# RWKV's inverse updates summed in PSUM and copied by ScalarE, its preparation off GpSimd, and its steps earlier in the layer's script

## What is computed

```
h = rms_norm(x, norm_g[i]); z = h @ w_in[i]
y_a = rwkv7_branch(z_a, ...)      # 6 heads of 64
y_b = dsa_branch(z_b, ...)        # 4 heads, keys chosen by top-k of an index score
y_c = dilated_branch(z_c, ...)    # 6 heads, three masks, one joint softmax
x = x + concatenate([y_a, y_b, y_c]) @ w_out[i]
...
# rwkv7: state step per token
sa = einsum('bhvk,bhk->bhv', state, -kk_t)
state = state * w_t + sa[..., None] * (kk_t * a_t) + v_t[..., None] * k_t
y_t = einsum('bhvk,bhk->bhv', state, r_t)
```

## Time and profile before

| what | value |
|---|---|
| median of 3 runs | 1381.98 us (1381.41 to 1382.36) |
| the profiled execution's own time | 1390.62 us |
| its span | 1388.8 us |
| PE, DVE, ACT, POOL busy | 85%, 69%, 49%, 10% of the span |
| mean granted clock of PE | 0.896 |
| layer 0 of the first block | from the start to about 241 us |
| layer 1 of the first block | about 308 to 529 us |

### The profile page before, as it was taken

How to read it: one execution, slowest core, us unless ns; L and a number is a source line. 1 busy time by engine, 2 the same in 40 slices (tenths; PEclk the granted TensorE clock), 3 DMA queues, 4 the chain that set the end, 5 groups by cost and what they waited for, 6 DMA issues and landing times.

```text
span 1388.8 us, 24893 instructions
## 1 busy us (share of the span) xinstructions
PE 1174.7 (85%) x10397; PEld 1089.9 (78%) x10397; DVE 957.5 (69%) x1729; ACT 675.3 (49%) x1224; POOL 139.9 (10%) x140
## 2 busy tenths in 40 slices
PE   7879876979799759859967799997979869999796
PEld 6868665978688648758955599996978849999696
DVE  5677865666877856676768667887547476788752
ACT  5543233456442234555437656655444364565541
POOL 2011000110110001151000011111011001011100
PEclk9889966989899878979968999998989869999898
DMA  8333200344242004315430054554534303455450
GB/s 331 120 102 107 93 2 1 130 144 152 89 149 92 2 1 167 127 71 208 141 114 1 17 193 156 183 171 170 177 123 175 125 1 122 152 183 169 154 179 31
DMA packets 24448, 167.55 MB, mean 121 GB/s; under 512 B 2704, under 2 KB 2832, under 8 KB 8336
## 3 DMA queue, kind: packets, MB, share of 16 engines
q1 hardware_dynamic: 24336, 165.96, 34.1%
HBM read 164.90 MB, written 1.05 MB: 119 GB/s over the span
## 4 chain that ended last, share of the span: by engine, by line
PE 46%; DVE 33%; ACT 14%; issue 5%; DMA 1%; POOL 1%; POOLq 0%; DVEq 0%; SPq 0%; ACTq 0%
DVE WL L381 8%; PE ps L427 8%; PE ps L424 7%; PE ps L422 7%; DVE ARENA L2031 5%; DVE FR L381 4%; ACT WH L368 3%; PE ps L445 3%; PE ps L453 3%; PE ps L447 3%; ACT ARENA L745 2%; PE ps L643 2%; ACT FR L368 2%; DVE ARENA L2023 2%; DMA raw<-wst_in 1%
## 5 line engine op out<-in xcount | busy, mean ns | idle before, releaser
L381 DVE TENSOR_TENSOR WL<-raw,WH 128x1024 fp32r<-128x1024 f32 (+4 forms) x225 | 269.5, 1219 | 145.5 <-ACT WH L368 144.9
L422 PE MATMUL ps<-FR,WH 128*128 128x256 f32 x1248 | 313.7, 290 | 29.1 <-ACT WH L368 15.3
L424 PE MATMUL ps<-FR,WH 128*128 128x256 f32 x1248 | 310.6, 288 | 2.6 <-POOL FR L501 0.9
L368 ACT ACTIVATE WH<-raw 128x1024 fp32r<-128x1024 f32 (+4 forms) x225 | 217.5, 989 | 122.0 <-PE ps L427 65.1
L422 PEld LDWEIGHTS ps<-FR,WH 128*128 128x128 f32 x1248 | 246.9, 198 | 35.0 <-ACT WH L368 11.3
L424 PEld LDWEIGHTS ps<-FR,WH 128*128 128x128 f32 x1248 | 246.4, 197 | 6.2 <-POOL FR L501 2.1
L427 PE MATMUL ps<-FR,WL 128*128 128x256 f32 x1248 | 175.1, 284 | 10.5 <-DVE WL L381 10.5
L422 PE MATMUL ps<-FR,FR 128*128 128x256 f32 x680 | 170.4, 287 | 8.9 <-ACT FR L497 7.4
L424 PE MATMUL ps<-FR,FR 128*128 128x256 f32 x680 | 169.6, 286 | 0.9 <-DVE FR L501 0.7
L427 PEld LDWEIGHTS ps<-FR,WL 128*128 128x128 f32 x1248 | 160.9, 195 | 11.2 <-DVE WL L381 11.2
L381 DVE TENSOR_TENSOR FR<-raw,FR 128x1024 fp32r<-128x1024 f32 (+2 forms) x100 | 117.4, 1193 | 75.6 <-ACT FR L368 75.5
(11 more groups left out here) (308 smaller groups left out, 1820.2 us busy)
## 6 DMA issues: line engine op xcount, KB each, us to landing
raw<-wst_in SPq DMA_DIRECT2D x123, 1024.0 KB, 5.0
raw<-wst_in SPq DMA_DIRECT2D x17, 896.0 KB, 4.6
raw<-wst_in SPq DMA_DIRECT2D x11, 768.0 KB, 4.3
raw<-wst_in SPq DMA_DIRECT2D x4, 912.0 KB, 4.6
cst<-cst_in SPq DMA_DIRECT2D x1, 1681.0 KB, 15.0
X<-xT_in SPq DMA_DIRECT2D x2, 512.0 KB, 6.2
ARENA<-memT_in SPq DMA_DIRECT2D x1, 1024.0 KB, 5.5
out_dram<-X SPq DMA_DIRECT2D x2, 512.0 KB, 2.6
```

Of the source, the lines that this page charges most:

```text
L368: a.activation(hi[:, 0:cols], src, ACT.Copy).then_inc(*put("split_hi", ("hi", i)))
L381: v.tensor_tensor(lo[:, 0:cols], src, hi[:, 0:cols].bitcast(F32), SUB).then_inc(*put("split_lo", ("lo", i)))
L422: pe.matmul(out, hv[:, k, :], src.hi[:, c, :], start=k0 == 0 and k == ks[0], stop=False)
L424: pe.matmul(out, hv[:, k, :], src.lo[:, c, :], start=False, stop=False)
```

## The change

1. Updates: for each T and U update PE first adds minus the identity times the old T (or U) into the same place of PSUM, then the product. ACT copies the sum out with scale -1. DVE's subtractions go. A constant `minus i64` of 64 columns is added, and the arena is 64 columns smaller.
2. POOL's three products of the preparation and its start of U (as two instructions per half, the first a product with -1 and the mask) go to DVE.
3. For jobs 0 to 7 of both layers ACT multiplies P by 1/l (an activation with that scale); the reciprocal stays on DVE.
4. RWKV has two more steps (one before the transposes for PE and ACT; on DVE the Newton steps, the products behind them, and the last products are steps of their own), and the script places them otherwise: 34 of the 43 stand in the written part, 9 between the attention jobs.

```diff
-                   rows 2 0, gact 1, R, rows 2 1, gact 2, R, rows 2 2, R, rows 2 3, R, rows 3 0, rout 2, R, rows 3 1, ropei, R, rows 3 2, R,
...
+                   rows 2 0, gact 1, R, R, rows 2 1, gact 2, R, rows 2 2, R, R, rows 2 3, R, rows 3 0, rout 2, R, rows 3 1, ropei, R, R,
...
 # attn_v
-            if j.turn == "A":
+            if j.turn == "A" and "times" not in j.more:
                 for p, l in j.scales():
                     v.tensor_scalar(p, p, l, None, MUL).then_inc(*put("attn_v", ("P", j.id)))
 # attn_a
-        if s == 2 and j.turn == "V":
+        if s == 2 and (j.turn == "V" or "times" in j.more):
 # rwkv_pe
+                for x in ("T", "U") if lv < 5 else ("U",):
+                    ps, old = begin_bank(x, l, lv, b), m.Tm if x == "T" else m.Um
                     for i in range(6):
+                        u = 6 * b + i
                         for h in HALVES:
+                            pe.matmul(ps[h, 64 * i:64 * i + 64], MINUS[h, :], old[h, u, :], start=True, stop=False)
+                        for h in HALVES:
+                            w, r0 = (m.Um, m.Wm) if x == "T" else (m.Wm, m.Um)
+                            ins = pe.matmul(ps[h, 64 * i:64 * i + 64], w[h, u, :], r0[h, u, :], start=False, stop=True)
 # rwkv_a
+                for x, to in (("T", m.Tm), ("U", m.Um)) if lv < 5 else (("U", m.Um),):
...
+                    a.activation(to[:, us, :], six(ps), ACT.Copy, scale=-1.0).then_inc(*put("rwkv_a", (x, l, lv, b), free))
 # rwkv_v
+        v.tensor_tensor(g_, g_, m.tmp, MUL).then_inc(*put("rwkv_v", ("g", l)))
         newton(v, q, "rwkv_v", m.tmp, m.tmp, 0.0, m.kq)
+        yield
+        v.tensor_tensor(m.bq, m.bq, m.E2, MUL).then_inc(*put("rwkv_v", ("bq", l)))
+        v.tensor_tensor(m.kr[:, :, 1, :], r_, m.cs, MUL).then_inc(*put("rwkv_v", ("rq", l)))
+            v.scalar_tensor_tensor(m.Um[:, us, :], m.Mb[:, us, 0:64], -1.0, bc(C("level0t"), 1, 6), MUL, MUL).then_inc(*put("rwkv_v"))
+            v.tensor_tensor(m.Um[:, us, :], m.Um[:, us, :], bc(I64, 1, 6), ADD).then_inc(*put("rwkv_v", ("U", l, 0, b)))
-                    v.tensor_tensor(m.Tm[:, us, :], m.Tm[:, us, :], six(ps), SUB).then_inc(*put("rwkv_v", ("T", l, lv, b), free))
-                v.tensor_tensor(m.Um[:, us, :], m.Um[:, us, :], six(ps), SUB).then_inc(*put("rwkv_v", ("U", l, lv, b), free))
```

More of the change, by code:

```diff
@@ L50, in const_table @@
     parts["i64"] = k == n64
+    parts["minus i64"] = -1.0 * (k == n64)
     def rows(m):
@@ L1149, in rwkv_a @@
         yield
-        for _ in range(10):
+        for lv in range(1, 6):
+            yield
+            for b in range(2):
+                us = slice(6 * b, 6 * b + 6)
+                for x, to in (("T", m.Tm), ("U", m.Um)) if lv < 5 else (("U", m.Um),):
+                    ps, free = psum(x, l, lv, b)
+                    q.wait_ge(*got(x + " pe", l, lv, b))
+                    if x == "U":
+                        q.wait_ge(*got("U", l, lv - 1, b))
+                    a.activation(to[:, us, :], six(ps), ACT.Copy, scale=-1.0).then_inc(*put("rwkv_a", (x, l, lv, b), free))
             yield
@@ L1268, in rwkv_v @@
         yield
+        for b in range(2):
+            us = slice(6 * b, 6 * b + 6)
+            q.wait_ge(*got("M", l, "b", b, 1))
+            q.wait_ge(*got("prep pe", l))
+            v.scalar_tensor_tensor(m.Um[:, us, :], m.Mb[:, us, 0:64], -1.0, bc(C("level0t"), 1, 6), MUL, MUL).then_inc(*put("rwkv_v"))
+            q.wait_ge(*own("rwkv_v"))
+            v.tensor_tensor(m.Um[:, us, :], m.Um[:, us, :], bc(I64, 1, 6), ADD).then_inc(*put("rwkv_v", ("U", l, 0, b)))
         yield
@@ L1359, in rwkv_g @@
         m = lm[l]
-        r_, gate = m.zm[:, 0:3, :], m.zm[:, 9:12, :]
-        yield
-        q.wait_ge(*got("sg g", l))
-        g_.tensor_tensor(gate, gate, m.tmp, MUL).then_inc(*put("rwkv_g", ("g", l)))
-        yield
-        for _ in range(4):
-            yield
-        q.wait_ge(*got("b", l))
-        q.wait_ge(*got("e2", l))
-        g_.tensor_tensor(m.bq, m.bq, m.E2, MUL).then_inc(*put("rwkv_g", ("bq", l)))
-        yield
-        q.wait_ge(*got("e1", l))
-        q.wait_ge(*got("z", l, 2))
-        g_.tensor_tensor(m.kr[:, :, 1, :], r_, m.cs, MUL).then_inc(*put("rwkv_g", ("rq", l)))
-        yield
-        for _ in range(7):
-            yield
-        for b in range(2):
-            us = slice(6 * b, 6 * b + 6)
-            q.wait_ge(*got("M", l, "b", b, 1))
-            q.wait_ge(*got("prep pe", l))
-            g_.tensor_tensor(m.Um[:, us, :], m.Mb[:, us, 0:64], bc(C("level0t"), 1, 6), MUL).then_inc(*put("rwkv_g"))
-            q.wait_ge(*own("rwkv_g"))
-            g_.tensor_tensor(m.Um[:, us, :], bc(I64, 1, 6), m.Um[:, us, :], SUB).then_inc(*put("rwkv_g", ("U", l, 0, b)))
-        yield
-        for _ in range(12):
+        gate = m.zm[:, 9:12, :]
+        for _ in range(30):
             yield
```

39 lines of the change are left out of this document (17 added, 22 removed).

## The result

| | before | changed |
|---|---|---|
| median of 7 runs each | 1382.36 us | 1391.57 us |
| the profiled execution's own time | 1390.62 us | 1392.93 us |
| its span | 1388.8 us | 1391.0 us |
| mean granted clock of PE in it | 0.896 | 0.911 |

The change is slower: ratio 1.0063, 95% interval 1.0039 to 1.0087. The forecast was 1379.5, and the result lies just above its range. The two profiled executions differ by 2.3 us only, the medians by 9. That gap is part of what has to be explained.

The account below looks back on a forecast made before the run. PE was taken to bound the row stretch, DVE what follows, with mutual waits in the tail. Layer 0 -3.9 and layer 1 +1.6 made -2.3, rounded to -2.5 us against the median: 1379.5, range 1370 to 1391.

Parts of the forecast that it names:

- to P1: Stretch up to the end of the product rows 3 0; forecast -7.5 us in layer 0, -6.5 in layer 1.
- early 0.7: Earlier in each layer, two DVE instructions under POOL's first product stop losing time: 0.7 us per layer taken.
- P4: Mark at the output product of job 4; before, at 235.3 us in layer 0 and 522.3 in layer 1.
- tail: From the first scores' eviction to job 4's output product: 40.4 us forecast, -11.6 in layer 0, -7.7 in layer 1.
- P3 to X: From the first scores' eviction to the start of what follows the layer; forecast -11.6 / -7.7, all before P4.
- P1 to P2: From rows 3 0's end to the last row product's: +12.6 us per layer for doubled matmul groups, +7.9 for moved steps.
- P2 to P3: From the last row product's end to the first scores' eviction: 15.1 us forecast, -5.3 in layer 0, -4.7 in layer 1.
- the lead: DVE takes POOL's preparation, low parts get fast: rows 3 0 ends 6.8 us earlier in layer 0, 5.8 in layer 1.
- sum of 15.1: Listed DVE and PE work with hops, from the last row product to the first scores' eviction: 15.1 us.
- The same stages make it up: Claim that the median, 8.6 us below the profiled execution, has the same stages, so the difference applies to the median.
- The matmuls: Rival: 25.2 us of new matmuls outweigh the tail's gain if ACT's queue becomes the chain; 1388 us, chance 0.18.
- The clock's mean: Rival: PE's clock stays up behind the last row product and in the tail; -10 to -13 us, 1370, chance 0.15.

Follow-up runs that it names:

- G: Kernel before with GpSimd's preparation (gate, b, r, start of U) moved to DVE alone, old order of steps: 1379.57 us, ratio 0.9968.
- U: The inverse's updates on PE and ACT (products with minus identity, ACT copies); alone on the kernel before: 1400.96 us, ratio 1.0125.
- GSO: Changed kernel with the update code of before; preparation on DVE, scaling of P on ACT and new order of steps kept: 1370.56 us, ratio 0.9904.
- the rotation first: GSO with the rotation and its transposes ahead of the last selection steps, those behind the first and second chunk's steps: 1371.5 us, ratio 0.9892.

## Why the prediction was wrong

The steps, against the means of two profiles of each kernel (layer 0 / layer 1, us; "to P1" holds the forecast's early 0.7; from P4 to X it had no change, so its tail stands against P3 to X):

| step | forecast | measured |
|---|---|---|
| to P1 | -7.5 / -6.5 | -10.9 / -7.3 |
| P1 to P2 | +20.5 / +20.5 | +21.2 / +21.1 |
| P2 to P3 | -5.3 / -4.7 | -2.2 / -1.7 |
| P3 to X | -11.6 / -7.7 | -9.2 / -7.2 |
| sum | -3.9 / +1.6 | -1.2 / +4.9 |

- **To P1: the lead was right, the rest was the early clock.** From Newton's end to P1 the gain is 7.5 and 6.6 us against 6.8 and 5.8 of the forecast, and POOL did make the low parts slow; but most of it (5 us) is the order's, and G alone brings 1 to 2.5. In layer 0 3.5 us more were there already before Newton's end (70.8 for 74.3), where the forecast had 0.7: the low clock at 39 to 46 and 56 to 60 us of before is gone (1.00 over the first 60 us for 0.91). Up to 2.6 us of that is luck, since one execution with the same instructions up to there had Newton's end at 73.4.
- **P1 to P2: right.** 18 groups at 0.66 measured for 0.70, and the moved steps at 9.3 for 7.9 (21.1 less 11.8).
- **P2 to P3: failed.** The sum of 15.1 began with the row output. In the trace a top-k stands ahead of it, 1.9 us from 173.3 to 175.3: an entry of the script, the selection's step behind the last row product, that the list left out. With it the stretch is at best 16.5, and DVE is busy for 15.3 us of that, where the list had 12.0 of DVE's own work and 2.1 of PE's. And it said the lower clock would cost 1.4; it costs 3.3, since the chunk and the scores lie in it too. Together 6.1 us over both layers.
- **P3 to X: nearly right, by a wrong split.** 2.9 us short. The head of the tail was right: the first Newton step came 7.3 and 7.5 us behind P3 for 7.6. What failed lies from there to P4, where the forecast had 32.8 us and the changed kernel 34.8 to 35.4. The scaling was to take 3.4 off there and took nothing beside U. Its 1.07 us was a price beside POOL, which the forecast itself said, next to a rule by which an instruction with one SBUF input goes on; the row contradicts that rule for this instruction. And the 52.0 us of layer 0 before were one execution's: the second has 48.6 from P3 to P4. "The same stages make it up" was the error behind this: the first profile had 3.6 us of low clock in the very stretch that the change shortens, and these were booked as a gain.
- **The sum against the median: failed.** Up to X of layer 1 the profiles' means differ by 3.7 us, in the whole time by 3.9, and the medians over all runs by 7.4 (1391.8 less 1384.4). The other 3.6 are the profiled executions of before, 1390.6 and 1386.4, above their median by 4.1 on average, and those of the changed kernel above theirs by 0.5. The forecast carried an offset of 8.6 us over to the changed kernel; there it was 1.4. In which stretches the shorter runs of before are shorter stays open, as no profile of one was taken. Their granted clock is higher over the whole run (0.908 in a run of 1381.5, 0.899 in one of 1390.7).
- **The rivals.** The matmuls do win, at +9 and not by ACT's queue: the tail shortened nearly as forecast, and P3 to P4 is 42.3 to 42.7 us in both profiles, under the 45 that the prediction set as that rival's sign. The clock's mean did rise (0.896 and 0.904 to 0.911 and 0.909), and what this gives is within the sum.
- **In short.** 1379.5 was off by 12.1 us: by 4.8 in the profiled execution (+2.3 for -2.5) and by 7.3 in the offset (1.4 for 8.6). In the first the list behind P2 alone is wrong by 6.1, and the luck ahead of P1 hid a part of it.

The best kernels are those without U ahead of P2: GSO at 1370.6 is 1.0% below before and 1.5% below the changed one; the rotation first (1371.5, ratio 0.9892) and the old order with U at the last levels (1372.8, 0.9912) can't be told from it. The new order with U at fewer levels was not tried.
